# Splitting each non-expert weight slab into its high and low part with one instruction per engine in place of two

## The reference

```
def first_block(...):      # rms_norm, x @ w_in, mlstm_mixer, nsa_mixer, gated merge @ w_branch, @ w_out, FFN
def second_block(...):
        h = _rmsnorm(x, g_mix[l])
        (gq, gk, gv, gg, ga, dq, dk, dv, iq, ik, iw, mq, gates) = _split_in(h @ w_in[l])
        ...
        merged = (gate[:, :, 0] * (o_gla @ w_o_gla[l])
                  + gate[:, :, 1] * (o_dsa @ w_o_dsa[l])
                  + gate[:, :, 2] * (o_mem @ w_o_mem[l]))
        x = x + merged @ w_out[l]
        x = x + _hier_moe(_rmsnorm(x, g_ffn[l]), ...)
```

## Time and profile before

| | us |
|---|---|
| median of 3 runs | 1071.64 |
| lowest and highest | 1070.89, 1072.2 |
| the profiled execution's own time | 1073.09 |
| its span, first to last instruction | 1071.8 |
| mean granted TensorE clock | 0.984 of full |

### The profile page before, as it was taken

How to read it: one execution, slowest core, us unless ns; L and a number is a source line. 1 busy time by engine, 2 the same in 40 slices (tenths; PEclk the granted TensorE clock), 3 DMA queues, 4 the chain that set the end, 5 groups by cost and what they waited for, 6 DMA issues and landing times.

```text
span 1071.8 us, 17772 instructions
## 1 busy us (share of the span) xinstructions
PE 1030.5 (96%) x7460; PEld 958.2 (89%) x7460; DVE 683.5 (64%) x1016; ACT 588.4 (55%) x880; POOL 37.0 (3%) x49
## 2 busy tenths in 40 slices
PE   5999998998999999999999999999999989999998
PEld 5999987798999999899999988999999977888886
DVE  3855664485556545765584555747555668989993
ACT  4645465545444343564475553775444457877781
POOL 5001000000000000000000000100000000000000
PEclk9999998999999999999999999999999989999999
DMA  9675442266656555555453343553465917999991
GB/s 288 202 238 156 119 119 79 79 198 185 204 195 195 181 179 193 173 182 173 148 163 119 119 122 120 189 167 119 158 197 182 318 51 258 364 355 365 367 331 40
DMA packets 181677, 203.25 MB, mean 190 GB/s; under 512 B 11287, under 2 KB 171646, under 8 KB 181598
## 3 DMA queue, kind: packets, MB, share of 16 engines
q1 hardware_dynamic: 171312, 195.63, 56.7%
q10 hardware_dynamic: 8958, 3.57, 1.4%
q0 software_dynamic: 1328, 2.92, 0.9%
HBM read 200.51 MB, written 2.63 MB: 190 GB/s over the span
## 4 chain that ended last, share of the span: by engine, by line
PE 92%; DVE 3%; DMA 2%; ACT 1%; ACTq 1%; issue 1%; POOL 0%; SPq 0%; DVEq 0%; POOLq 0%
PE bank L578 77%; PE bank L685 2%; DMA rev_copies<-rev_rows 1%; PE bank L733 1%; PE bank L723 1%; PE bank L2729 1%; DMA ring<-in_w_in 1%; PE bank L2785 1%; PE bank L2436 1%; PE bank L2352 1%; DVE w_lo L554 1%; ACTq L1116 1%; PE bank L2498 1%; PE bank L2453 1%; PE bank L2633 0%
## 5 line engine op out<-in xcount | busy, mean ns | idle before, releaser
L554 DVE TENSOR_TENSOR w_lo<-ring,w_hi 128x1024 fp32r<-128x1024 f32 (+1 forms) x304 | 425.5, 1435 | 195.4 <-ACT w_hi L546 194.3
L546 ACT ACTIVATE w_hi<-ring 128x1024 fp32r<-128x1024 f32 (+1 forms) x304 | 359.7, 1226 | 155.8 <-PE bank L578 94.9
L578 PE MATMUL bank<-xT_hi,w_hi 128*128 128x256 f32 x896 | 256.5, 286 | 0.0
L578 PE MATMUL bank<-xT_lo,w_hi 128*128 128x256 f32 x896 | 253.9, 283 | 0.0
L578 PE MATMUL bank<-xT_hi,w_lo 128*128 128x256 f32 x896 | 253.6, 283 | 0.0
L578 PEld LDWEIGHTS bank<-xT_hi,w_hi 128*128 128x128 f32 x896 | 171.2, 191 | 3.2 <-issue 2.5
L578 PEld LDWEIGHTS bank<-xT_lo,w_hi 128*128 128x128 f32 x896 | 171.3, 191 | 0.6 <-issue 0.2
L578 PEld LDWEIGHTS bank<-xT_hi,w_lo 128*128 128x128 f32 x896 | 171.2, 191 | 0.0
L578 PE MATMUL bank<-w_hi,xT_hi 128*128 128x256 f32 x368 | 105.2, 286 | 3.8 <-ACT kT L1184 3.8
L578 PE MATMUL bank<-w_lo,xT_hi 128*128 128x256 f32 x368 | 103.5, 281 | 0.0
L578 PE MATMUL bank<-w_hi,xT_lo 128*128 128x256 f32 x368 | 103.3, 281 | 0.0
(11 more groups left out here) (512 smaller groups left out, 1893.2 us busy)
## 6 DMA issues: line engine op xcount, KB each, us to landing
ring<-in_w_in SPq DMA_DIRECT2D x55, 1024.0 KB, 5.3
ring<-in_w_down SPq DMA_DIRECT2D x31, 1024.0 KB, 7.5
ring<-in_w_gate SPq DMA_DIRECT2D x40, 512.0 KB, 5.7
ring<-in_w_up SPq DMA_DIRECT2D x40, 512.0 KB, 7.9
ring<-in_w_gate SPq DMA_DIRECT2D x11, 1024.0 KB, 5.4
ring<-in_w_up SPq DMA_DIRECT2D x11, 1024.0 KB, 5.4
ring<-in_w_out SPq DMA_DIRECT2D x8, 1024.0 KB, 5.1
ring<-in_w_mem_kv SPq DMA_DIRECT2D x8, 1024.0 KB, 5.8
```

Of the source, the lines that this page charges most:

```text
L546: act.activation(HIGHS[HI_SLOT[s]][:, k, :], RAWS[SLOT[s]][:, k, :], ACT.Copy).then_inc(w_hi_ready, 1)
L554: vec.tensor_tensor(LOWS[SLOT[s]][:, k, :], RAWS[SLOT[s]][:, k, :], HIGHS[HI_SLOT[s]][:, k, :].bitcast(F32), ALU.subtract).then_inc(w_lo_r ...
L578: ins = pe.matmul(dst, a, b, start=(start and j + m == 0), stop=(stop and j == len(pairs) - 1 and m == 2), **kw)
```

## The change

The halves are gone: for all slabs ACT makes `w_hi` with one instruction of 2048 elements a partition and DVE makes `w_lo` with one; slab s has count s + 1 on both semaphores. PE waits once before a slab, for the whole `w_lo`, and the wait of the second half is removed. The places at which slabs are split, the slots, the loads and the matmuls stay as they are.

```diff
-    def halves(s):
-        return (slice(0, KT // 2), slice(KT // 2, KT)) if s < MOE else (slice(0, KT),)
-    def parts_of(s, n):
-        return 2 * s + n + 1 if s < MOE else MOE + s + 1
     def high(act, end):
...
-            for k in halves(s):
-                act.activation(HIGHS[HI_SLOT[s]][:, k, :], RAWS[SLOT[s]][:, k, :], ACT.Copy).then_inc(w_hi_ready, 1)
+            act.activation(HIGHS[HI_SLOT[s]], RAWS[SLOT[s]], ACT.Copy).then_inc(w_hi_ready, 1)
     def low(vec, end):
         for s in range(split["lo"], end):
-            for n, k in enumerate(halves(s)):
-                vec.wait_ge(w_hi_ready, parts_of(s, n))
-                vec.tensor_tensor(LOWS[SLOT[s]][:, k, :], RAWS[SLOT[s]][:, k, :], HIGHS[HI_SLOT[s]][:, k, :].bitcast(F32),
-                                  ALU.subtract).then_inc(w_lo_ready, 1)
+            vec.wait_ge(w_hi_ready, s + 1)
+            vec.tensor_tensor(LOWS[SLOT[s]], RAWS[SLOT[s]], HIGHS[HI_SLOT[s]].bitcast(F32),
+                              ALU.subtract).then_inc(w_lo_ready, 1)
     def slab_in(pe, s):
-        pe.wait_ge(w_lo_ready, parts_of(s, 0))
+        pe.wait_ge(w_lo_ready, s + 1)
-    def second_half(pe, s):
-        pe.wait_ge(w_lo_ready, parts_of(s, 1))
     def slab_rows(...):
-                if n == 0 and k == max(start, KT // 2):
-                    second_half(pe, s)
     def slab_tokens(...):
-            if t == 0 and k == KT // 2:
-                second_half(pe, s)
         def down(e):
-            second_half(pe, s)
```

## The result

In its first five runs the changed kernel took 1076.73 us, the median, between 1075.31 and 1078.89. The kernel before took 1071.64 (1069.75 to 1073.85, five runs). The ratio is 1.0049, 95% interval 1.0032 to 1.0065: slower, by 5.1 us where 1.9 was forecast, and outside the range. The profiled execution took 1078.89 us, its span is 1077.6 at a mean granted clock of 0.981 (before 1073.09, 1071.8 and 0.984).

A forecast was written before the change was run, and what follows sets the result against it. PE, busy 1030.5 of 1071.8 us, was taken as the bound, with ACT and DVE felt only where PE waits for them. The place-by-place terms summed to +1.9 us, giving 1073.5 us from the median 1071.64; range 1071.3 to 1075.7.

The forecast's parts named there:

- step 7: Everywhere else, including FFN, GLA and second merge: no cost, since delayed results have enough cover, 1 us or more in FFN.
- 90 us more of waiting for `w_hi`: Expected sign on DVE: its wait for ACT's high parts up by about 90 us while the time moves by 2.
- Step 2: Slab 9: the whole low part ends later and PE waits for it instead of `kT`, +0.2 us.
- Step 3: Slab 10: its later low part delays `v_sw` behind it on DVE, which PE needs, +0.2 us more.
- Steps 1 and 4: Start, low part of slab 0: -0.06 us; ACT's copies of the mLSTM state at 118 us: -0.05 us.
- Step 5: Merge of the first block: slab 24's low part delays the `mixT_lo` chain PE waits for, +0.67 us.
- Step 6: DSA attention: slabs 102 and 103 delay DVE's results and PE's transposes of units 1 and 2, together +0.93 us.
- The rival on the clock: Added PE pauses lower the clock, 1.7 us more, 1075.2 us; chance 0.18 together with another turn of the DSA loop.
- a new stretch at half clock: Sign of being wrong: PE's granted clock has a stretch at half that the profile before lacked.

The follow-up runs named there:

- e9: Kernel before with ACT's high parts in halves, DVE's low parts whole and one PE wait per slab: 1074.43 us, ratio 1.0023.
- e10: Kernel before with ACT's high parts whole, DVE's low parts in halves behind them, PE waiting twice: 1073.41 us, ratio 1.0027.
- e8: Kernel before with ACT and DVE still in halves, only PE's two waits per slab made one: 1070.91 us, ratio 0.9998.
- e6: The changed kernel run again without edit, twelve runs, against the kernel before: 1073.23 us, ratio 1.0022.
- e3: Kernel before with only slabs 9 and 10 whole: 1072.32 us, ratio 1.0003.
- e4: Kernel before with only slabs 24, 63, 102 and 103 whole: 1073.46 us, ratio 1.0027.
- e12: Kernel before with only slabs 24, 63, 102 and 103 whole, run a second time: 1073.29 us, ratio 1.0016.
- e5: The kernel before, unchanged, run as if it were a changed one: 1072.20 us, ratio 1.0000.
- e11: The changed kernel run a third time without edit, twelve runs, against the kernel before: 1073.61 us, ratio 1.0011.
- e7: Kernel before with slabs 9, 24, 63, 102 and 103 in four parts instead of two: 1071.24 us, ratio 0.9996.

## Why the prediction was right or wrong, point by point

- *The step that failed* is step 7, "elsewhere nothing", and with it that the sum and its error put the clock at nothing. Of the 5.8 us between the two profiled executions 0.45 lies at the place that step 7 left out, and some 3.5 in stretches at half clock, which neither the sum nor its 0.6 of error covers. In the median of the first five runs it is alike: their mean clock of 0.9824 against 0.9854 is worth 2.5 of the 5.1 us by the slope. The one sum that had the clock in it, the rival's, allowed 1.7 us for a single stretch.
- *The mechanism* held for the rest: the whole low part ended 4.23 us after its high part's start (4.24 in the text), and the cost stands where other results are queued behind a low part on DVE. e9 and e10 show that the lost overlap is the cause, e8 that PE's waits are free. The forecast of 90 us more of waiting for `w_hi` was wrong (47).
- *Step 2, slab 9* (+0.2): +0.16, `w_lo` in the place of `kT`. The load's landing moved the pause by more than that, from execution to execution (3.8 to 4.95 us over all profiles).
- *Step 3, slab 10* (+0.2): +0.24 to +0.26 in e6 and e3, where PE came in time; nothing where PE was slower through slab 9, at half clock.
- *Steps 1 and 4*: within 0.1 us of the -0.11 expected.
- *Step 5, merge* (+0.67): 0.49 to 0.52 at block 4 and 0.05 at block 6 in the changed kernel, 0.68 with slab 24 alone. Right.
- *Step 6, DSA* (+0.93): mis-sized for the changed kernel as profiled. It is 0.14 + 0.49 = 0.63, and in an execution with a long issue of `slot_no` and slabs 102 and 103 whole 1.0 to 1.4 (e4, e12). The prediction was read from an execution with a long issue, and for such a one it is near. The cover of 0.37 us on which the step rested was that of one execution; in e5 it is 1.4. And with a short issue the chain begins at slab 100, not at 102.
- *Step 7, "elsewhere nothing"*: failed. Slab 63's low part with `memT_lo` behind it makes the residual sum late by 0.3 to 0.45 us. The row was there to be read: before, DVE began that sum right when PE ended the FFN, having been idle for only 0.25 us, which is less than 0.79. The prediction's sentence that in the FFN the delayed results have 1 us or more is wrong here.

```profile
442.96 3.22 DVE L699 SCALAR_TENSOR_TENSOR memT_lo<-bank,cols,memT_hi 128x256 fp32r<-128x256 f32 x8
446.43 2.48 DVE L1913 TENSOR_TENSOR x<-bank,x 128x512 f32<-128x512 f32 x4 [0.25 <-PE bank L578]
```

- *Sum*: 1.9 forecast, 1.6 to 1.9 read, 2.5 +- 0.4 by the runs. That it agrees is partly luck: the errors of steps 6 and 7 cancel.
- *The range*: 1071.3 to 1075.7 against 1076.73. It was built from the terms, with the clock taken as fixed unless the change's pauses moved it. But 35 runs of before in a set reach from 1069.0 to 1075.0, and the changed kernel from 1070.6 to 1077.1 in its later sets. The medians of those sets, 1073.23 and 1073.61, lie within the range. Three runs of before, 1.3 us apart, were taken for the spread.
- *The rival on the clock* named the right thing. That the change's pauses are its cause isn't shown, nor is it ruled out (e9). What the traces show is that the stretches at half clock can lie differently in two executions of one program. The prediction named a new stretch at half clock as a sign of being wrong, and the first profile had several; but so has one execution of a kernel against another. e6 and e11 are both the changed kernel at a mean clock of 0.986, and their spans are 1075.8 and 1072.0: between the matmuls at 155 and at 172 us of e11 e6 loses 4.3 us to it, with the clock at 0.50 from 170 us on where e11 has 1.00:

```profile
170.00:173.50 3.50, 3.50 (x16) 2.49 (x15) 2.34 (x8) 0.80 (x3) 0.00 (x0) 0.50 0.02 5
```

  The experts' wait for `hidden` (2.5 us against 0.9) belongs here too: e7 and e8, which have no whole slab before the experts, have it as well. Where PE runs the gate products at the full clock (a matmul each 0.23 us) it then waits longer for `hidden`; where it runs them at half clock (0.43 us) the wait is short. The Trainium skill's page "TensorE: Matmul & The Clock Gate", Part 1, says that the point of the clock's first rise depends on where the first matmul lands in something that doesn't start with the kernel. It says this of the rise, not of later falls; if it holds for them too, such differences need no cause in the program, and e6 and e11, one program with different stretches, agree with that. Why all of the first five runs had a low clock (0.981 to 0.984, mean 0.9824 against 0.9861 in the next 24) isn't settled.

## What to carry to other kernels

Two half instructions on two engines are a pipeline: making them one saves little (here 3 to 4% from start to end, 7 to 9% by durations) and gives up the overlap. That delays the second engine each time it is already waiting, and what pays is what stands *behind* that instruction in its queue. List for every such place the result next in the queue and its cover, including sums and transposes of other stages. And take the cover, and the spread for a range, from several executions: here loads landed 1 us apart, and one DMA issue on ACT took 2.2 or 3.2 us, in the same program. Where single runs differ by more than the effect, as here, the first five executions can't size it.

## What the runs showed of the hardware

- The issue of the `slot_no` load on ACT's queue took 2.1 to 2.3 us in twelve profiles and 3.1 to 3.7 in eight, and held ACT for as long; two executions of the same kernel differ in it.
- The kernel before ran from 1068.9 to 1076.2 us, with mean granted clocks from 0.981 to 0.989. Equal mean clock doesn't mean equal time: it matters where the stretches at half clock fall (3.8 us between e6 and e11).
- The granted clock fell to half right behind PE's pause at the end of the FFN in one profile (e9, 448.1 to 451.5 us, 1.5 us lost) and not in the ten others with the same or a like pause.
- On ACT as on DVE one instruction over 128x2048 (1915 and 2292 ns) is barely shorter than two over 128x1024 from start to end (2.00 and 2.35 us).
